# Moving the SBUF homes of the front slot, em_h, em_l and en_l in a fused two-block transformer kernel

## The reference, cut to what matters

```
for layer in range(2):
    x = layer_norm(ALPHA * x + mixer(x))        # even_mixer, then odd_mixer
    x = layer_norm(ALPHA * x + memory_cross_attention(x, mem))
    x = layer_norm(ALPHA * x + swiglu(x))       # 1024 -> 2 x 2816 -> 1024
for layer in range(2):
    x = layer_norm(ALPHA * x + 0.5 * swiglu(x))
    x = layer_norm(ALPHA * x + mixer_sublayer(x))
    x = layer_norm(ALPHA * x + memory_cross_attention_2(x, mem_2))
    x = layer_norm(ALPHA * x + 0.5 * swiglu(x))
```

## Time and profile before

| | |
|---|---|
| median of 3 runs | 2230.66 us (2228.38 to 2231.65) |
| the profiled execution's own time | 2233.17 us |
| its span, first to last instruction | 2231.4 us |
| TensorE busy | 2203.0 us, 99% of the span |
| VectorE, ScalarE busy | 1435.2 us, 1074.0 us |
| mean granted TensorE clock | 0.995 |

### The profile page before, as it was taken

How to read it: one execution, slowest core, us unless ns; L and a number is a source line. 1 busy time by engine, 2 the same in 40 slices (tenths; PEclk the granted TensorE clock), 3 DMA queues, 4 the chain that set the end, 5 groups by cost and what they waited for, 6 DMA issues and landing times.

```text
span 2231.4 us, 38216 instructions
## 1 busy us (share of the span) xinstructions
PE 2203.0 (99%) x16007; PEld 2047.8 (92%) x16007; DVE 1435.2 (64%) x1678; ACT 1074.0 (48%) x1320; POOL 118.4 (5%) x206
## 2 busy tenths in 40 slices
PE   9999999999999999999999999999999999999998
PEld 8989899888989989998999998998998999998997
DVE  6885655577655555556876676556556876677555
ACT  4554444357454443443556464443443555555442
POOL 2300000020000000000011000000000002000000
PEclk9999999999999999999999999999999999999999
DMA  8756555674645665566454655565565554564553
GB/s 245 217 180 207 170 184 191 191 210 143 207 151 184 195 226 170 189 218 199 151 157 143 201 196 180 190 217 180 190 203 190 181 168 154 158 233 158 189 180 122
DMA packets 349595, 413.92 MB, mean 185 GB/s; under 512 B 12013, under 2 KB 281513, under 8 KB 349297
## 3 DMA queue, kind: packets, MB, share of 16 engines
q1 hardware_dynamic: 339232, 377.19, 52.8%
q0 software_dynamic: 10192, 34.29, 5.0%
HBM read 406.44 MB, written 5.00 MB: 184 GB/s over the span
## 4 chain that ended last, share of the span: by engine, by line
PE 91%; DVE 5%; DMA 1%; ACT 1%; issue 1%; SPq 0%; POOL 0%; DVEq 0%; ACTq 0%
PE bank L360 91%; DMA raw<-in_even_w_in 1%; DVE wl L1850 0%; DVE x L1964 0%; DVE qkT L2133 0%; DVE z L1959 0%; DVE stat L1925 0%; DVE front_l L1850 0%; ACT wh L1291 0%; DVE z L1923 0%; DMA lamt<-in_odd_lambda 0%; DVE em_l L1850 0%; ACT em_h L1291 0%; DVE qkT L2131 0%; SPq L2749 0%
## 5 line engine op out<-in xcount | busy, mean ns | idle before, releaser
L1850 DVE TENSOR_TENSOR wl<-raw,wh 128x2048 fp32r<-128x2048 f32 (+2 forms) x344 | 759.0, 2212 | 506.5 <-ACT wh L1291 423.7
L360 PE MATMUL bank<-xl,wh 128*128 128x256 f32 x3144 | 877.4, 279 | 6.0 <-issue 5.2
L360 PE MATMUL bank<-xh,wl 128*128 128x256 f32 x3144 | 871.1, 277 | 0.0
L360 PE MATMUL bank<-xh,wh 128*128 128x256 f32 x3144 | 870.9, 277 | 0.0
L1291 ACT ACTIVATE wh<-raw 128x2048 fp32r<-128x2048 f32 (+2 forms) x344 | 634.9, 1850 | 317.3 <-PE bank L360 299.1
L360 PEld LDWEIGHTS bank<-xl,wh 128*128 128x128 f32 x3144 | 591.5, 188 | 13.3 <-issue 11.2
L360 PEld LDWEIGHTS bank<-xh,wl 128*128 128x128 f32 x3144 | 591.5, 188 | 0.6
L360 PEld LDWEIGHTS bank<-xh,wh 128*128 128x128 f32 x3144 | 591.3, 188 | 0.2
L360 PE MATMUL bank<-wl,hh 128*128 128x512 f32 x528 | 205.9, 390 | 0.0
L360 PE MATMUL bank<-wh,hh 128*128 128x512 f32 x528 | 205.5, 389 | 0.0
L360 PE MATMUL bank<-wh,hl 128*128 128x512 f32 x528 | 205.4, 389 | 0.0
(11 more groups left out here) (395 smaller groups left out, 3157.6 us busy)
## 6 DMA issues: line engine op xcount, KB each, us to landing
raw<-in_ffn_w_in SPq DMA_DIRECT2D x80, 1024.0 KB, 5.2
raw<-in_w_mix_in SPq DMA_DIRECT2D x56, 1024.0 KB, 5.3
raw<-in_ffn_w_gu SPq DMA_DIRECT2D x40, 1024.0 KB, 5.2
raw<-in_ffn_w_out SPq DMA_DIRECT2D x40, 1024.0 KB, 5.1
raw<-in_ffn_w_down SPq DMA_DIRECT2D x20, 1024.0 KB, 5.1
raw<-in_mem_wkv SPq DMA_DIRECT2D x16, 1024.0 KB, 5.4
raw<-in_even_w_in SPq DMA_DIRECT2D x12, 1024.0 KB, 6.5
raw<-in_w_branch SPq DMA_DIRECT2D x24, 512.0 KB, 3.6
```

Of the source, the lines that this page charges most:

```text
L360: ins = pe.transpose(o, a, b) if transpose else pe.matmul(o, a, b, start=start, stop=stop)
L1850: dve.tensor_tensor(part_of(t, 1)[:, half:], raw_tile(t)[:, half:], part_of(t, 0)[:, half:].bitcast(F32), ALU.subtract).then_inc(sig("w_lo ...
```

## The change

It moves the five small tensors from behind `pc` to before `front_h` and adds a gap of 64 bytes behind them; it takes the gap before `em_h` away and puts one of 64 bytes before `en_h`; and it makes the other gaps so wide that `hh`, `hl`, `mh`, `ml`, `mem_n`, `xq`, `xk`, `xv` and `en_h` stay where they were. No instruction is added, taken away or moved.

```diff
@@ -112,6 +112,12 @@
     gb = sb("gb", [P, 2, D])
     ident = sb("ident", [P, P])
     ones = sb("ones", [P, P])
+    stat = sb("stat", [P, TB, 4, 6])
+    mv = sb("mv", [P, TB, 4])
+    nmax = sb("nmax", [P, 2, 4])
+    psum_e = sb("psum_e", [P, 2, 4])
+    rden = sb("rden", [P, 2, 4])
+    sb("gap_front", [P, 16])
     st = ExitStack()
     front_h = sb("front_h", [P, TILE], F32R, st)
     front_l = sb("front_l", [P, TILE], F32R, st)
@@ -124,22 +130,17 @@
     pc = sb("pc", [P, P])
-    stat = sb("stat", [P, TB, 4, 6])
-    mv = sb("mv", [P, TB, 4])
-    nmax = sb("nmax", [P, 2, 4])
-    psum_e = sb("psum_e", [P, 2, 4])
-    rden = sb("rden", [P, 2, 4])
...
-    sb("gap_hh", [P, 48], F32, st)
+    sb("gap_hh", [P, 32], F32, st)
...
-    sb("gap_mh", [P, 32], F32, st)
+    sb("gap_mh", [P, 16], F32, st)
@@ -148,11 +149,11 @@
-    sb("gap_em", [P, 32], F32, st)
     em_h = sb("em_h", [P, TILE], F32R, st)
     em_l = sb("em_l", [P, TILE], F32R, st)
+    sb("gap_em", [P, 16], F32, st)
     en_h = sb("en_h", [P, TILE], F32R, st)
-    sb("gap_en", [P, 3 * 2048 + 1040], F32, st)
+    sb("gap_en", [P, 3 * 2048 + 1136], F32, st)
     en_l = sb("en_l", [P, TILE], F32R, st)
```

## The result

| | before | after |
|---|---|---|
| median of 5 executions each | 2230.61 us | 2253.53 us |
| ratio | | 1.0104 (95% interval 1.0089 to 1.0119) |
| span of the profiled execution | 2231.4 us | 2249.7 us |
| TensorE busy | 2203.0 us | 2221.2 us |

One of the five executions after took 5682.33 us and is left out of the ratio; without it their median is 2252.8 us. So the change costs 22 to 23 us. The forecast was 2231.6 us with a range up to 2247.

The account below looks back on a forecast made before the run. TensorE, busy 2203.0 of 2231.4 us, was taken to bound the kernel. The terms -1.2 -0.1 -1.3 -0.3 +3.8 gave +0.9, called +1.0 us: a median of 2231.6 us, range 2224 to 2247.

Parts of the forecast that it names:

- Where to look: Whole kernel: only SBUF homes change, so only the distance of matmul starts and who makes TensorE wait can move time.
- Part 1: Front's 288 matmuls 256 wide, offset +64 to -64: 1.2 us less at 113.4 ns, 0 in the slower beat.
- Part 2: Front's 72 matmuls 512 wide: 0.1 us less, bounds 0.1 less to 0.3 more.
- Part 3: em over x, offset 0 to -64: 1.3 us less (0.5 in the loose beat), plus at most 0.3 less.
- Part 4: en's 3 x 64 matmuls, only en_l moved to -64: no change, bounds 0.9 us less to 0.4 more.
- Part 5: yh and yl over w, 576 matmuls, offset -64 to 0: 3.8 us more, bounds 0 and 3.8.
- The case that homes don't matter: Rival C, whole kernel: the homes have no effect, 2230.7 us; chance 0.15.
- Part 6: All other moved homes, fp32 products and transposes: 0, with 0.3 us either way.
- Part 7: VectorE and ScalarE writing to new homes, the subtraction among them: 0.
- rival A: ffn streams behind front lose the tight beat, 3.5 us a sublayer: about 2247 us with four, 2254 with six; chance 0.30.
- A's mechanism: At the seam behind front, x over w at the same offset inherits front's loose beat and keeps it for 864 matmuls.

Follow-up runs that it names:

- experiment 8: The kernel before with xh and xl alone moved up 64 bytes to remainder 128, offset 0 to w: 2285.08 us, ratio 1.0246.
- experiment 3: The changed kernel with iw, 64 bytes, moved behind yl, so that y is back at remainder 64: 2252.33 us, ratio 1.0096.
- experiment 6: The changed kernel with front moved to remainder 64, offset 0 to x: 2248.17 us, ratio 1.008.
- experiment 11: The kernel before with front alone moved from remainder 128 to 192: 2254.2 us, ratio 1.0111.
- experiment 9: A separate program rebuilding the opening behind a cross sublayer with the kernel's homes, varying em's and front's: x over w behind took 113.3 or 117.8 ns a matmul.
- experiment 10: The changed kernel with front moved to remainder 160, offset 96 to x: 2232.4 us, ratio 1.0016.
- experiment 2: The changed kernel with front alone back at remainder 128: 2239.12 us, ratio 1.0043.
- experiment 5: A separate program of 174 streams 256 wide and 16 of 512 wide, varying offset, place and entry: 113.3 ns in 31 of 31 at offsets 112 and 368.

## Why the prediction was wrong, point by point

- **Where to look** (only homes change, so only beats can): right but for 0.8 us of waits. Same counts, same busy time of VectorE and ScalarE.
- **Part 1, front +64 to -64, 1.2 us less**: not so. The tight beat came in the two blocks of one opening, elsewhere 117.8; of the -2.88 us in the sums 2.7 are the clock of before's execution.
- **Part 2, front 512 wide**: +0.28 us, the upper bound, where I had taken -0.1.
- **Part 3, em**: -0.4 us instead of -1.6; it landed mostly in the loose beat, for which the same part had 0.5.
- **Part 4, en**: +0.06. Right.
- **Part 5, y, +3.8**: +3.58 measured, -3.6 when undone. Right, from em's row at offset 0 alone. The case that homes don't matter was the wrong one for this kernel: experiment 8 measures 56.6 us from the home of x alone. The Trainium skill, "SBUF — State Buffer", section "Who interferes with whom", says that PE never waits on anyone; it speaks of engines in each other's way and has nothing on homes, so by the measurement it can't be read as "homes don't matter".
- **Part 6, the other moved homes, 0 with 0.3 either way**: wrong by more than its bound. The four x over w tiles of the merges lost 1.64 us in every run with these homes; the rows that the part rests on are those of the moved operands' own products, not of the streams behind them.
- **Part 7**: the subtraction is as before, but two waits behind probT over ckn grew by 0.8 us. In experiment 3 only 0.2 of it is left, with the home of y and of the tensors between iw and y.
- **The step that failed** is a term that the sum does not have: the ffn streams, 864 matmuls of x over w in each of six sublayers, were given the tight beat unchanged. The case in which they lose it, rival A, got 0.30, with the range cut at four of six streams. All six lost it: 22.95 us by the sums, 3.83 each where A had 3.5, since the loose beat of x over w is 117.8 and not the 117.5 of mem's row. I had seen that the beat changes at the seam (loose front, then 113.4) and that -64 shows both beats; "no seam of these six goes wrong today" is no argument once front has a new offset. To split A into four and six was sound: experiment 6 has just the four behind a cross sublayer loose. That all six went here was not to be had from the rows, and a range that is to hold A has to end at six, 2254.
- **A's mechanism** was right in place and price and wrong in its inside. Not a beat that is handed on: in the opening at 271.78 us front was tight and x over w loose, and experiment 11 has front in neither. What the runs show is that the homes of the tiles ahead of the seam pick the beat of the stream behind it (experiments 9, 10, 11), and at some homes what ran still earlier does too (experiments 2 and 5). That a phase is what carries this over the seam is an interpretation; no run shows a phase itself.

Open: what in the hardware carries it, why 256 bytes, why experiment 2 loses the stream at 873.0 us, and which of the small homes costs the four tiles in the merges their beat.

## What to carry to other kernels

Where a profile shows one shape of matmul in several beats, divide last minus first start by the count for every stream, and list the remainder of both blocks modulo 256: the pair of homes is a tuning size of its own, worth 2.5% here. Before a tile is moved, ask what streams right behind it without a break: here a hoped-for gain of 0.1 us in 24 matmuls stood against a loss of 3.8 in the 864 that follow. A short program with the same sequence of homes foretold experiments 10 and 11, but not experiment 2, at a home where the kernel itself gave both beats. So a home that was good in every history tried (front at 160: six streams of the kernel, eight cases of the program) is worth more than one with the best beat of its own.

## What was not expected of the hardware

- The distance of matmuls 256 wide in this type depends on both operands' homes: 113.3 to 120.0 ns at steps of 16 bytes, repeating every 256 bytes; moving x by 64 bytes made 9,432 of them 54.7 us longer.
- At offsets 64 and -64 there are two steady beats, 113.3 and 117.8, kept over 864 matmuls; with em at 64, front at 96, 128, 160 or 224 leaves the stream **behind** front tight, at 0, 32, 64 or 192 loose.
- One beat only, 113.3, at offset 112 in 31 of 31 streams with the stationary block at multiples of 64, but 120.0 at offset 112 modulo 256 with it at 240.
- 512 wide: 226.6 to 234.4 ns by offset.
